# A constant's square root ahead of a wait, and a reciprocal ahead of the state's decay, in a chunked scan

## The reference, cut to what matters

```
def step(carry, inp):                      # over the 4 chunks
    st, dec = inp
    return dec[..., None, None] * carry + st, carry
...
y = y_diag + y_off + d_skip * xs           # inside a chunk, from the state, skip
y = y * silu(z)
y_ssd = rmsnorm(y, ssd_norm)               # y / sqrt(mean(y*y) + 1e-6) * gain
return concatenate([y_ssd, y_pool]) @ w_out
```

## Time and profile before

| what | value |
| --- | --- |
| time, median of 3 runs | 1671.44 us |
| the profiled execution: its time | 1672.18 us |
| its span | 1670.5 us |
| TensorE busy | 1644.4 us (98%) |
| VectorE, ScalarE, GpSimd busy | 941.1, 564.8, 1052.8 us |
| granted TensorE clock | 0.999 of full speed |

### The profile page before, as it was taken

One profiled execution on the slowest core, in us unless ns is written; L12 is line 12 of the kernel. 1 busy time (PEld: TensorE's weight loads), 2 busy tenths in 40 slices (PEclk: granted clock), 3 DMA queues, 4 the chain that ended last, 5 costly groups with the idle time before them and its releaser, 6 DMA issues.

```text
span 1670.5 us, 22260 instructions
## 1 busy us (share of the span) xinstructions
PE 1644.4 (98%) x8071; PEld 1361.8 (82%) x8071; DVE 941.1 (56%) x1435; ACT 564.8 (34%) x981; POOL 1052.8 (63%) x776
## 2 busy tenths in 40 slices
PE   7999999999999999999999999999999999999998
PEld 5898997888978888888888888887887778877887
DVE  5323948772445221221237998999657686656624
ACT  5431247330422100100135445674312245555301
POOL 7675764466647666776665788785469644334664
PEclk9999999999999999999999999999999999999999
DMA  6333333223233333323234332222242322111231
GB/s 209 126 103 123 105 102 126 80 98 101 94 134 101 100 101 97 88 93 101 88 104 111 101 101 89 82 83 77 76 152 83 101 76 65 63 51 51 76 107 70
DMA packets 188330, 162.36 MB, mean 97 GB/s; under 512 B 7636, under 2 KB 184400, under 8 KB 187728
## 3 DMA queue, kind: packets, MB, share of 16 engines
q1 hardware_dynamic: 188040, 161.10, 30.5%
q10 hardware_dynamic: 200, 0.06, 0.0%
HBM read 155.87 MB, written 4.23 MB: 96 GB/s over the span
## 4 chain that ended last, share of the span: by engine, by line
PE 91%; DVE 5%; ACT 2%; issue 1%; POOL 1%; DMA 0%; DVEq 0%; SPq 0%; ACTq 0%
PE g_bank L901 65%; PE g_bank L918 7%; PE g_bank L928 5%; PE t_bank L1496 2%; PE g_bank L1383 1%; PE t_bank L1508 1%; PE t_bank L1219 1%; PE t_bank L1251 1%; PE t_bank L1485 1%; PE t_bank L1301 1%; PE t_bank L1322 1%; PE g_bank L1068 1%; PE g_bank L1365 1%; PE t_bank L962 1%; PE t_bank L1476 1%
## 5 line engine op out<-in xcount | busy, mean ns | idle before, releaser
L761 POOL TENSOR_TENSOR w_lo<-w_raw,w_hi 128x512 fp32r<-128x512 f32 x388 | 540.2, 1423 | 8.1
L744 POOL TENSOR_SCALAR w_hi<-w_raw 128x2048 fp32r<-128x2048 f32 x98 | 192.8, 1967 | 484.5 <-issue 204.7
L901 PE MATMUL g_bank<-x_hi,w_hi 128*128 128x512 f32 x1232 | 489.0, 397 | 0.4 <-DVEq L2288 0.2
L901 PE MATMUL g_bank<-x_hi,w_lo 128*128 128x512 f32 x1232 | 479.9, 390 | 0.0
L901 PE MATMUL g_bank<-x_lo,w_hi 128*128 128x512 f32 x1232 | 479.7, 389 | 0.0
L901 PEld LDWEIGHTS g_bank<-x_hi,w_hi 128*128 128x128 f32 x1232 | 231.4, 188 | 51.1 <-issue 4.8
L901 PEld LDWEIGHTS g_bank<-x_hi,w_lo 128*128 128x128 f32 x1232 | 231.3, 188 | 48.8
L901 PEld LDWEIGHTS g_bank<-x_lo,w_hi 128*128 128x128 f32 x1232 | 231.5, 188 | 47.6 <-issue 1.4
L2714 DVE SCALAR_TENSOR_TENSOR t_bank<-hc,cols,t_bank 128x512 f32<-128x512 f32 x280 | 187.0, 749 | 4.7 <-DVE hc L2698 2.8
L811 POOL TENSOR_TENSOR w_lo<-w_raw,w_hi 128x512 fp32r<-128x512 f32 x104 | 134.3, 1326 | 68.1 <-ACT w_hi L1933 68.1
L901 PE MATMUL g_bank<-y_hi,w_hi 128*128 128x512 f32 x332 | 130.9, 394 | 0.0
(11 more groups left out here) (493 smaller groups left out, 2890.9 us busy)
## 6 DMA issues: line engine op xcount, KB each, us to landing
w_raw<-w_gate_up SPq DMA_DIRECT2D x44, 512.0 KB, 4.9
w_raw<-a_w_in SPq DMA_DIRECT2D x44, 512.0 KB, 4.3
w_raw<-b_w_in SPq DMA_DIRECT2D x38, 512.0 KB, 4.0
w_raw<-w_in SPq DMA_DIRECT2D x28, 512.0 KB, 4.5
w_raw<-w_kv SPq DMA_DIRECT2D x16, 512.0 KB, 4.3
w_raw<-w_out_mix SPq DMA_DIRECT2D x16, 512.0 KB, 6.2
w_raw<-w_down SPq DMA_DIRECT2D x16, 512.0 KB, 3.9
w_raw<-a_w_out SPq DMA_DIRECT2D x16, 512.0 KB, 3.9
```

The lines of the kernel that those rows point to most:

```text
L744: nc.gpsimd.tensor_scalar(w_hi[:, par], w_raw[:, par], 1.0, 0.0, ALU.mult, ALU.add).then_inc(pool_chain, 1)
L761: last = nc.gpsimd.tensor_tensor(w_lo[:, par, s], w_raw[:, par, s], w_hi[:, par, s].bitcast(F32), ALU.subtract)
L901: last = nc.tensor.matmul(g_bank[:, 2 * pair + f, 0:n], ww[:, k0 + k, ws], xk, start=(k == 0 and q == 0), stop=(k == kt - 1 and q == 2))
```

## The change

ScalarE takes the root of a constant, `eps`, after the decays and ahead of its wait for the chunk, in chunks 1 to 3. The result goes to the place that the chunk's own root overwrites. On VectorE the wait for the root and the reciprocal become a function, which is called before the state's decay in chunk 0 and after it, as before, in the other chunks.

```diff
                 if c < CHUNKS - 1:
                     decay(c + 1)
+                if c:
+                    link(nc.scalar.activation(ysum[:, c, 1:2], eps[:, 0:1], ACT.Sqrt))
                 act.wait_ge(y_ready, c + 1)
...
+                def root_reciprocal():
+
+                    dve.wait_ge(ysq_ready, c + 1)
+                    v.reciprocal(ysum[:, c, 0:1], ysum[:, c, 1:2]).then_inc(yr_ready, 1)
+
+                if c == 0:
+                    root_reciprocal()
                 if c < CHUNKS - 2:
...
                     link(v.tensor_tensor(state_into(c + 2), state_into(c + 1), decay, ALU.mult))
-                dve.wait_ge(ysq_ready, c + 1)
-                v.reciprocal(ysum[:, c, 0:1], ysum[:, c, 1:2]).then_inc(yr_ready, 1)
+                if c:
+                    root_reciprocal()
```

## The result

The changed kernel takes 1678.49 us (median of 6 runs, 1677.53 to 1678.98) against 1672.06 us for the kernel before (6 runs): ratio 1.0037, 95% interval 1.0027 to 1.0047. It is 6.4 us slower, where 0.5 us were forecast, and lies outside the predicted range. The executions of the kernel before fall into two groups about 1 us apart (1671.43 to 1671.68 and 1672.43 to 1672.54), so a few tenths between two medians say little.

The account below looks back on a forecast made before the run. TensorE, busy 98% of the span, was taken as the bound. The terms -1.46 + 3.13 - 0.79 - 0.41 = +0.47 us on the median of 1671.44 gave 1671.9 us, range 1669.7 to 1673.2.

Parts of the forecast that it names:

- All that the scan can give is 2.66 us: TensorE's turns of chunks 0, 1 and 2 are late by 1.46, 0.79 and 0.41 us, the most the edit can gain.
- The reciprocal ahead of the decay, and the decay behind GpSimd's part: Chunk 0: reciprocal at 263.35 instead of 265.04, the turn's 1.46 us wait gone, decay still ending at 265.00.
- The split meets the scores, 1.67 us: Chunk 1: GpSimd's earlier weight split (L744) holds the second scores half, making VectorE 1.67 us later.
- From there VectorE's x_lo, the bank, the second yoff matmul and all of TensorE's chunk 1 are 1.67 us later: VectorE's 1.67 us delay passes unchanged to TensorE, which comes to chunk 1's turn at 286.34.
- No case reaches that: No forecast case differs from no change by 0.2%, 3.3 us; chance of a time within 0.2%: 0.94.
- The table load ahead of the wait: Chunks 1 to 3: ScalarE's load and added root fit its idle time, cost nothing; turn waits of 0.79 and 0.41 us go.
- Chunk 3 and all that follows keep the shift: From chunk 2's turn on, TensorE stays 0.47 us later than before, to the end of the span.

Follow-up runs that it names:

- e5_decay_early: The whole change, with chunk 0's state copied and decayed in VectorE's waits ahead of the scan: 1669.83 us against 1672.36 before, ratio 0.9985.
- e3_split_held: The whole change, but GpSimd's split for the third slice of wo_pool also waits for chunk 1's scores: 1670.41 us, ratio 0.9987 to the kernel before.
- e4_filled: The whole change, with TensorE computing state(1) three times in the time it idled: 1672.09 us against 1672.37 before, ratio 0.9999.
- e1_root_only: The kernel before with only ScalarE's early root, VectorE's order unchanged: 1670.82 us against 1672.37 before, ratio 0.9989.
- e2_recip_only: The kernel before with only chunk 0's early reciprocal, no early root: 1679.23 us against 1672.37 before, ratio 1.0039.
- e7_held_late: e3_split_held with two reciprocals of a dead buffer on VectorE behind chunk 1's scores: median 1672.20 us, executions 1671.61 to 1676.86, ratio 1.0005.
- e8_held_later: e7_held_late with three reciprocals instead of two behind the scores: median 1678.86 us, ratio 1.0033 to the kernel before.
- e9_before_later: e6_before_late with four reciprocals instead of two behind the scores: median 1674.55 us, ratio 1.0021 to the kernel before.
- e6_before_late: The kernel before, with two reciprocals of a dead buffer on VectorE behind chunk 1's scores: 1673.19 us, ratio 1.0004.

## Why the prediction was wrong, point by point

- *All that the scan can give is 2.66 us*: e5_decay_early shows 2.5 us (2.23 in the scan of its trace, 54.99 for 57.22); the reading of the late turns was right.
- *The reciprocal ahead of the decay, and the decay behind GpSimd's part*: right. The decay took 1.56 us instead of 2.31 and ended where it did before, as worked out.
- *The split meets the scores, 1.67 us*: right. The first x_lo comes 1.64 us later than before (270.15 for 268.51), and e3_split_held removes the meeting and with it the loss.
- *"From there VectorE's x_lo, the bank, the second yoff matmul and all of TensorE's chunk 1 are 1.67 us later. TensorE comes to chunk 1's turn at 284.67 + 1.67 = 286.34"*: here the prediction failed. The yoff matmul came at the time given, but the step then let TensorE run on at its old speed, as if an idle of 3.1 us cost 3.1 us. After this idle the granted clock was 0.50 until 286 us, and the turn came at 292.70. The missing term is 6.4 us in the trace, 6.7 us by e4_filled. The profile of before showed no fall of the clock after its idle of 1.30 us, and no rival had one; "No case reaches that", said of the 0.2%, followed from this. The Trainium skill ("TensorE: Matmul & The Clock Gate", section "Why this matters for your kernels") advises against long idle of TensorE between bursts of matmuls, since the clock falls back to its lower level; this trace agrees, 0.50 after 3.12 us.
- *The table load ahead of the wait*: right. For e1_root_only 1.2 us were expected; it is 1.5 by the medians and 1.15 in the scan of its trace (56.07 us for 57.22, counted as in e3_split_held). In the changed kernel it brought little, since TensorE itself was late at chunk 1: with it the loss is 6.4 us, without it (e2_recip_only, 1679.23 for 1672.37) 6.9.
- *Chunk 3 and all that follows keep the shift*: nearly. Chunk 2's turn is 6.77 us later than before (311.55 for 304.78), and the span ends 6.3 us later.

The profile of before does hold a sign of the missing term, at its start. TensorE idles 9.50 us there, does one matmul, and idles 2.37 us more. These rows stand in the stream that follows:

```profile
16.19 0.63 PE L1068 MATMUL g_bank<-x_lo,w_hi 128*128 128x512 f32 x1
16.62 0.63 PE L1068 MATMUL g_bank<-x_hi,w_lo 128*128 128x512 f32 x1
...
17.42 0.40 PE L1068 MATMUL g_bank<-x_lo,w_hi 128*128 128x512 f32 x1
17.66 0.39 PE L1068 MATMUL g_bank<-x_hi,w_lo 128*128 128x512 f32 x1
```

The starts are 0.43 us apart and then 0.24, nearly the two spacings of the changed kernel at half and at full clock (0.43 and 0.23). The profile prints a granted clock of 1.00 there, so the spacing is the only sign, and no run tests it.

What stays open is what decides whether the clock falls after an idle such as that of e7_held_late, and how long it then stays low. In the traces it is low for 13.6 us (changed kernel, e2_recip_only, e7_held_late, e8_held_later) or for 3.4 us (e9_before_later). The other executions have no trace. Judged by their times and mean granted clocks, e7_held_late, e8_held_later and e9_before_later have both long falls (0.995 or 0.996) and short ones or none (0.998, 0.999), an estimate: 13.6 us at half clock take 0.004 off the mean, 3.4 us take 0.001. The change itself lost its 6 us in all six executions, e2_recip_only in all five. The same page of the Trainium skill (section "What's actually happening") says that the window over which the chip watches TensorE's activity runs free and does not restart with the kernel, so that the point at which the clock changes varies between runs; the spread would fit that, and no run here separates it from other causes.

## What to carry to other kernels

When TensorE is nearly always busy, an engine wait that is worked out as some microseconds of idle on it has to be priced twice: by its length, and by the half clock that may follow. An edit that takes a wait away moves the idle to the next thing that TensorE needs, and a wait of 1.3 us that cost no more than itself became one of 3.1 that halved the clock. Before pulling such an engine forward, look at what its earlier end starts on another engine: here a weight split that excluded VectorE's two-input instructions, and with the scores issued first (e5_decay_early) a loss of 6.4 us became a gain of 2.5.

## What the runs showed of the hardware

- An idle of TensorE of 3.1 us halved its granted clock for 13.6 us in the changed kernel; one of 1.44 us in e3_split_held did not, nor did 1.30 and 1.16 us in e6_before_late; 2.62 us in e7_held_late did in some executions, and 1.30 and 2.33 us in e9_before_later did for 3.4 us.
- The clock fell about at the end of the idle or after it: 1.1 us after TensorE's next matmul in the changed kernel, 1.3 us after it in e7_held_late, 0.1 us ahead of it in e9_before_later. TensorE was busy nearly throughout the 13.6 us and the clock stayed low.
- Matmuls whose results are thrown away, put into the idle (e4_filled), kept the clock at 1.00 and gave back the whole 6.4 to 6.7 us.
- A GpSimd split that waited while one VectorE instruction with two SBUF inputs ran went ahead of the next VectorE instruction of that kind, though that one followed at once: issued at 267.31 behind a split issued at 266.92, the second scores half ended at 270.22, 1.06 us after the split (a free one takes 1.22), and the two halves took 4.04 us for 2.35.
